# Seven block products in place of eight in the first feed-forward product, residual and hidden layer in DRAM, index scores between projection steps

## What is computed

```python
score = einsum('bqhs,bqh->bqs', relu(einsum('bqhd,bsd->bqhs', q_idx, k_idx)), w_idx)   # 4 index heads of 64
_, sel = top_k(where(causal, score, -inf), 256)
...
h = h + merged @ w_out[i]
n2 = _rmsnorm(h, g_mlp[i])
h = h + square(relu(n2 @ w_ff1[i])) @ w_ff2[i]        # w_ff1 1024 x 4096, w_ff2 4096 x 1024
n3 = _rmsnorm(h, g_ple[i])
h = h + sigmoid(n3 @ w_ple_gate[i]) * (p[i] @ w_ple[i])
```

## Times and profile before

| | us |
|---|---|
| median of three runs | 1805.27 (1805.12 to 1806.44) |
| the profiled execution, its own time | 1806.59 |
| its span, first to last instruction | 1804.8 |

### The profile page before, as it was taken

How to read it: one execution, slowest core, us unless ns; L and a number is a source line. 1 busy time by engine, 2 the same in 40 slices (tenths; PEclk the granted TensorE clock), 3 DMA queues, 4 the chain that set the end, 5 groups by cost and what they waited for, 6 DMA issues and landing times.

```text
span 1804.8 us, 21895 instructions
## 1 busy us (share of the span) xinstructions
PE 1724.0 (96%) x8728; PEld 1362.2 (75%) x8728; DVE 808.2 (45%) x1321; ACT 559.3 (31%) x818; POOL 354.8 (20%) x166
## 2 busy tenths in 40 slices
PE   5899989999899999999998999999999999999997
PEld 4568778787556666678887888888888888888886
DVE  7499999901255576654323412121212222215524
ACT  5422322222355566621222302031211112114223
POOL 2212342122200000212211222222222222222220
PEclk8999999999899999999999999999999999999999
DMA  4202122242100020014320111111111111111112
GB/s 149 79 24 59 35 71 93 82 128 74 47 1 1 1 71 1 2 54 153 120 93 31 46 53 47 46 46 46 46 56 49 46 46 46 46 47 52 42 58 93
DMA packets 90324, 103.08 MB, mean 57 GB/s; under 512 B 15920, under 2 KB 82480, under 8 KB 90256
## 3 DMA queue, kind: packets, MB, share of 16 engines
q1 hardware_dynamic: 87504, 92.70, 16.5%
q10 hardware_dynamic: 2592, 9.44, 1.4%
q0 software_dynamic: 160, 0.02, 0.1%
HBM read 86.54 MB, written 13.76 MB: 56 GB/s over the span
## 4 chain that ended last, share of the span: by engine, by line
PE 90%; DVE 4%; ACT 3%; issue 1%; POOL 1%; DMA 0%; ACTq 0%; DVEq 0%; POOLq 0%
PE ps L1479 73%; PE ps L1697 3%; PE ps L1711 3%; PE ps L1662 2%; PE ps L1681 2%; PE ps L1668 2%; PE ps L1576 2%; PE ps L1776 1%; DVE sc L1174 1%; DVE prob_a L1303 1%; PE ps L1638 1%; DVE prob_b L1303 1%; DVE tmp L1450 0%; PE ps L1507 0%; POOL w_lo L660 0%
## 5 line engine op out<-in xcount | busy, mean ns | idle before, releaser
L660 POOL TENSOR_TENSOR w_lo<-w_raw,w_hi 128x1024 fp32r<-128x1024 f32 x131 | 315.7, 2411 | 1115.8 <-ACT w_hi L744 1115.8
L744 ACT ACTIVATE w_hi<-w_raw 128x1024 fp32r<-128x1024 f32 x131 | 138.7, 1061 | 929.5 <-PE ps L1479 883.1
L1479 PE MATMUL ps<-n_hi,w_hi 128*128 128x512 f32 x1120 | 351.3, 395 | 23.3 <-DVE n_lo L1372 6.6
L1479 PE MATMUL ps<-n_lo,w_hi 128*128 128x512 f32 x1120 | 349.0, 393 | 0.0
L1479 PE MATMUL ps<-n_hi,w_lo 128*128 128x512 f32 x1120 | 348.5, 393 | 0.0
L1479 PEld LDWEIGHTS ps<-n_hi,w_hi 128*128 128x128 f32 x1120 | 212.8, 191 | 71.3 <-issue 11.1
L1479 PEld LDWEIGHTS ps<-n_lo,w_hi 128*128 128x128 f32 x1120 | 213.1, 190 | 45.0
L1479 PEld LDWEIGHTS ps<-n_hi,w_lo 128*128 128x128 f32 x1120 | 212.8, 190 | 44.8
L1401 DVE TENSOR_TENSOR h<-h,ps 128x2048 f32<-128x2048 f32 x32 | 73.2, 2287 | 221.6 <-PE ps L1479 221.6
L1187 DVE TENSOR_SCALAR_CACHE_REDUCE tested<-sc,bar_i 128x384 bf16<-128x384 f32 (+2 forms) x192 | 169.0, 942 | 1.7 <-POOL sc L675 0.6
L1479 PE MATMUL ps<-hid_lo,w_hi 128*128 128x512 f32 x512 | 157.6, 389 | 0.0
(11 more groups left out here) (261 smaller groups left out, 2025.8 us busy)
## 6 DMA issues: line engine op xcount, KB each, us to landing
w_raw<-in_w_ff_dram SPq DMA_DIRECT2D x64, 512.0 KB, 3.5
w_raw<-in_w_in_dram SPq DMA_DIRECT2D x28, 512.0 KB, 3.7
gates_scratch<-stage ACTq DMA_DIRECT2D x16, 512.0 KB, 2.6
sig_ab<-gates_scratch SPq DMA_DIRECT2D x8, 1024.0 KB, 5.9
x_tok<-in_x_dram SPq DMA_DIRECT2D x8, 512.0 KB, 10.1
w_raw<-in_w_out_dram SPq DMA_DIRECT2D x8, 512.0 KB, 4.9
xs<-in_x_dram SPq DMA_DIRECT2D x4, 1024.0 KB, 5.0
w_raw<-in_w_ple_gate_dram SPq DMA_DIRECT2D x8, 512.0 KB, 3.4
```

Source lines behind the costliest of these rows:

```text
L660: pool.tensor_tensor(w_lo[s][:, :, :], w_raw[s][:, :, :], w_hi[s][:, :, :].bitcast(F32), ALU.subtract).then_inc(lo_ready, 1)
L744: act.activation(w_hi[s][:, :, :], w_raw[s][:, :, :], ACT.Copy).then_inc(hi_ready, 1)
L1479: last = pe.matmul(bank(4 * half + 2 * j + t)[0:w, :], wm, xm[:, t * HALF:(t + 1) * HALF], start=(k == 0 and a), stop=(k == total - 1 and ...
```

## The change

1. **First feed-forward product.** The input channels are divided into even and odd row tiles, a unit of 256 hidden columns into two column tiles, the tokens into two halves. A unit is so a 2 x 2 block product, and it is done with seven products of blocks in place of eight. A product (P1 to P7) is 4 row tiles x 3 matmuls over 512 tokens. Block sums of the weights (`s_raw`, four for each unit) and of the activations (T1 to T4, once) are made on VectorE and, for unit 0, on GpSimd. P1, P6, P7 and P4 accumulate one after another in bank 0 of the unit's half of PSUM, and ScalarE copies what stands there after P1, P6 and P7 (`copy_chain`). P2 lies in bank 1, P5 and P3 in bank 2. VectorE adds the copies to the other banks (`add_c11`, `add_c22`, `add_c12`) and applies relu and the norm's factor; C21 is taken from bank 0 after P4 (`take_c21`). Products of neighbouring units are interleaved in the order of `PRODUCTS`.
2. **Order of the feed-forward.** All 16 units of the first product run first; each hidden tile is squared and stored to DRAM (`hid_d`). Then the second product runs in eight passes of four groups, loading four hidden tiles for each pass, two buffers of four, and splitting them into high and low (`hid_high`, `hid_low`).
3. **Residual.** Each quarter of h is written to DRAM (`h_d`) after the output projection and read back before the second product. The load of p, its transposes and their parts move behind the first pass of the second product. The buffers of high, low and raw parts lie at other places of SBUF.
4. **Index scores.** One unit is now at most 512 keys of one pair of heads in its own two banks; after each of the units 1 to 16 comes a sixteenth (`qa_step`, 6 matmuls) of the first of the four projections. A high part is made ahead of the second sine, one at unit 12 and one after the scores; a low part ahead of the last mask.

The core of the diff (in this order: scratch tensors and product order, SyncE, GpSimd, ScalarE, VectorE, TensorE's index scores, TensorE's first product):

```diff
+    h_d = nc.dram_tensor("h_scratch", (D // P, P, S), F32, kind="Internal").ap()
+    hid_d = nc.dram_tensor("hid_scratch", (FF // P, P, S), F32, kind="Internal").ap()
...
+        UNITS_1 = FF // WCOL
+        B11, B21, B22, T1, T2, T3, T4 = range(7)
+        SECOND = {"P1": B11, "P2": B21, "P3": B22, "P4": T4, "P5": T1, "P6": T2, "P7": T3}
+        PRODUCTS = [(0, "P1"), (0, "P2"), (1, "P1"), (1, "P2"), (0, "P6"), (0, "P5"), (0, "P7"), (1, "P6"), (0, "P4"),
+                    (0, "P3"), (1, "P5"), (1, "P7"), (2, "P1"), (2, "P2"), (1, "P4"), (1, "P3")]
+        for u in range(2, UNITS_1):
+            PRODUCTS += [(u, "P6"), (u, "P5"), (u, "P7")]
+            PRODUCTS += [(u + 1, "P1"), (u + 1, "P2")] if u + 1 < UNITS_1 else []
+            PRODUCTS += [(u, "P4"), (u, "P3")]
...
+            for u in range(2, UNITS_1 + 1):
+                sp.wait_ge(a_lo_done, POS[u - 2, "P4"] + 1)
+                wait_sum(sp, u - 2, 4)
+                if u < UNITS_1:
+                    load_unit(u)
+                else:
+                    load_ff2(0)
+                    load_ff2(1)
+                if u >= 3:
+                    store_unit(u - 3)
+            sp.wait_ge(a_used, POS[UNITS_1 - 1, "P2"] + 1)
...
+            store_unit(UNITS_1 - 1)
+            sp.wait_ge(a_used, LAST)
+            sp.wait_ge(c12_done, UNITS_1)
+            for b in range(2):
+                sp.wait_ge(hid_stored[b], 32 * (UNITS_1 // 2))
...
+            load_h(0)
+            for k in range(CHUNK):
+                load_hid(1, k)
+            for q in range(1, 2 * OUT_N):
+                load_h(q)
             sp.dma_start(p_tok[:, :, :], p2.rearrange("(t q) d -> q t d", q=P)).then_inc(p_loaded, 16)
...
+            for n in range(2, 4 * FFN):
+                if n % 4 == 2 and 1 <= n // 4 < FFN - 1:
+                    sp.wait_ge(slab_used, FF2_SLAB + 4 * (n // 4))
+                    for k in range(CHUNK):
+                        load_hid(n // 4 + 1, k)
+                load_ff2(n)
...
+            def first_lo(o):
+                pool.wait_ge(a_hi_done, o + 1)
+                pool.tensor_tensor(a_lo[o % 10][:, :, :], first_of(o), a_hi[o % 10][:, :, :].bitcast(F32),
+                                   ALU.subtract).then_inc(a_lo_done, 1)
...
+            pool.tensor_tensor(s_raw[0][:, :, :], block_of(0, "A21"), block_of(0, "A22"), ALU.add).then_inc(s_first, 1)
...
+                    act.activation(n_pair[:, c, :], tile_ps(half, c), ACT.Copy,
+                                   scale=g_mlp_c[:, 2 * q + c:2 * q + c + 1]).then_inc(n_done, 1)
...
+                    act.activation(gated[:, :, :], hp[:, :, :], ACT.Square).then_inc(h_sq, 1)
+                    act.dma_start(h_d[2 * q:2 * q + 2].rearrange("a q n -> q a n"), hp[:, :, :]).then_inc(h_spilled, 16)
...
+            HI_AT = {0: (6,), 4: (7, 8), 5: (9, 10), 6: (11,), 7: (12, 13)}
+            for o, (u, name) in enumerate(PRODUCTS):
+                if name in ("P1", "P6", "P7"):
...
+                    copy_chain(u, name)
+                for ahead_o in HI_AT.get(o, ()) if o < 8 else (o + 6,):
...
+                        first_hi(ahead_o)
+                if o == 7:
+                    act.wait_ge(sq_summed, 1)
...
+                        act.activation(rms[:, t * HALF:(t + 1) * HALF], bank(4 * t + 3), ACT.Sqrt, bias=eps_c,
+                                       scale=1.0 / D).then_inc(root_done, 1)
+                if name == "P3" and u < UNITS_1 - 1:
+                    hid_square(u, 1)
+                if o >= 1 and PRODUCTS[o - 1][1] == "P3":
+                    hid_square(PRODUCTS[o - 1][0], 0)
...
+            add_c11(0)
+            sums_of_blocks(1)
+            add_c11(1)
+            add_c22(0)
+            inverse(2)
+            relu(0, 0, first, c11_done)
+            relu(1, 0, first, c11_done)
+            relu(0, 1, second, c22_done)
+            last_sum(1)
+            take_c21(0)
+            add_c12(0)
+            relu(0, 0, second, c12_done)
+            sums_of_blocks(2)
...
+            for u, (i, pair, c, w) in enumerate(IDX_UNITS):
...
+                if u >= 2:
+                    pe.wait_ge(rel_done, 2 * (u - 1))
...
+                if 1 <= u <= 2 * DT:
+                    qa_step(u - 1)
+            pe.wait_ge(rel_done, 2 * len(IDX_UNITS))
+            for _ in range(3):
                 project()
...
+            PLACE = {"P1": 0, "P6": 0, "P7": 0, "P4": 0, "P2": 1, "P5": 2, "P3": 2}
...
+                    if name in ("P1", "P2", "P5") and u >= 2:
+                        pe.wait_ge({"P1": c21_done, "P2": c11_done, "P5": c12_done}[name], u - 1)
+                    if name in ("P6", "P7", "P4"):
+                        pe.wait_ge(u_copied, COPY_AT[u, {"P6": "P1", "P7": "P6", "P4": "P7"}[name]] + 1)
+                    if name == "P3":
+                        pe.wait_ge(c22_done, u + 1)
...
+                    for w, x, a, z in ((a_hi, b_hi, True, False), (a_hi, b_lo, False, False), (a_lo, b_hi, False, True)):
+                        last = pe.matmul(unit_bank(u, PLACE[name]), w[o % 10][:, j, :], x[j][:, b, :],
...
+            for o in range(4):
+                first_product(o, range(0, KT - 1))
+            for o in range(4):
+                first_product(o, range(KT - 1, KT))
+            for o in range(4, LAST):
+                first_product(o, range(0, KT))
+                if o == 6:
+                    square_sums((3, 7), SQ3)
```

More of the change, by code:

```diff
@@ L1029, in out_weights @@
-            def out_weights():
+            for i in range(FFN):
                 for q in range(4):
                     hi_parts(1)
-                    at_.group(1)
-            root(1)
-            hidden(0, 0)
-            out_weights()
-            with act.Fori(0, FFN - 2) as i:
-                at_.loop(i, 8, 6)
-                ahead.loop(i, 8)
-                hidden(i, 1)
-                out_weights()
-                at_.end(FFN - 2)
-                ahead.end(FFN - 2)
-            hidden(0, FFN - 1)
@@ L1057, in _ @@
+                if i == 0:
+                    half = group()
+                    act.activation(pt_hi[:, :, :].rearrange("q a n -> q (a n)"), bank(4 * half, 4), ACT.Copy).then_inc(
+                        pt_hi_done, 1)
+            root()
             for q in range(2 * OUT_N):
@@ L1515, in _ @@
             project(((0, P),))
-            for half in range(2):
-                freed(pe, half, at_.groups // 2)
+            half = group()
+            freed(pe, 1 - half, (at_.groups) // 2)
             for t in range(TT):
@@ new lines, in _, with first_project, sums @@
+            for o in range(4):
+                first_product(o, range(0, KT - 1))
+            for o in range(4):
+                first_product(o, range(KT - 1, KT))
[3 more added lines that the diff above has]
+                    square_sums((3, 7), SQ3)
+            def first_project():
+                half = group()
+                g = at_.groups
+                def sums():
+                    freed(pe, g % 2, free_count(g - 2))
+                    square_sums((4 * (g % 2), 4 * (g % 2) + 1), SQ3 + DT)
+                product(half, FULL, (KT, KT), residual, first_wait=lambda k: pe.wait_ge(norm_lo, k + 1),
+                        after=lambda k: sums() if k == DT - 3 else None)
+                pe.wait_ge(root_done, 3)
@@ new lines, in ff2_product @@
+            def ff2_product(i, q):
+                half = group()
+                if i == 0 and q < 2:
+                    u = UNITS_1 - 2 + q
+                    pe.wait_ge(c11_done, u + 1)
+                    pe.wait_ge(c12_done, u + 1)
+                    pe.wait_ge(c21_done, u + 1)
+                product(half, FULL, (KT,), lambda k: (hid_hi[i % 2][k][:, :], hid_lo[i % 2][k][:, :]),
+                        first_wait=(lambda k: pe.wait_ge(hid_lo_done, CHUNK * i + k + 1)) if q == 0 else None)
@@ L1818, in feed_forward @@
+            assert at_.slabs == FF2_SLAB and (at_.groups - OUT_GROUP) % 2 == 0
+            for i in range(FFN):
                 for q in range(4):
+                    ff2_product(i, q)
+                if i == 0:
                     half = group()
-                    product(half, FULL, (KT,), lambda k: (hid_hi[:, k, :], hid_lo[:, k, :]),
-                            first_wait=hid_there if q == 0 else None)
-            feed_forward(0, 0)
-            with pe.Fori(0, FFN - 1) as i:
-                at_.loop(i, 8, 6, 6)
-                feed_forward(i, 1)
-                at_.end(FFN - 1)
+                    pe.wait_ge(p_loaded, 16)
+                    for f in range(2):
+                        for t in range(TT):
+                            last = pe.transpose(bank(4 * half + 2 * f, 2)[:, t * P:(t + 1) * P],
+                                                p_tok[:, t, f * P:(f + 1) * P], ident[:, :])
+                    last.then_inc(turn_done, 1)
```

586 lines of the change are left out of this document (408 added, 178 removed).

## The result

| | us | ratio to the kernel before, 95% interval |
|---|---|---|
| before, beside it (4 runs) | 1805.86 (1805.12 to 1806.90) | |
| changed kernel (4 runs) | 1783.42 (1781.77 to 1784.99) | 0.9875 [0.9858, 0.9892] |
| forecast | 1773.0 (1755 to 1789) | 0.982 |

The change gains 22.4 us; 32.2 were forecast. The time lies in the range of 1755 to 1789, but above the 1766 to 1780 that the forecast called its own. Of the rivals, (d) with 1782 is nearest: scores that gain nothing and a longer root stop.

A forecast was written before the change was run, and what follows sets the result against it. TensorE, 96% busy, was taken as the bound: fewer matmuls less new stops take the feed-forward stage from 708.6 to 680.9 us. 1806.59 - 27.7 - 4.5 = 1774.4, 1.3 less against the median: 1773, range 1755 to 1789.

The forecast's parts named there:

- (d): Rival: the index scores gain nothing and the root stop in the first feed-forward product doubles; 1782 us, chance 8%.
- (b): Rival: chain copies come late in the first product's steady units, 1 us in each of 14 units; 1787 us, 14%.
- Fewer matmuls: First feed-forward product: 84 matmuls per unit in place of 96, 192 fewer over 16 units, -43.5 us.
- their pace: First product's matmuls stay at 0.2267 us each; 12 in a row to one bank cost nothing extra, bounds 0 and 8 us.
- the steady units: First product: a unit lasts 19.0 us; the other engines' work, chain copies and transfers fit beside TensorE.
- (c): Rival: 12 matmuls in a row to one bank run slower; at 50 ns more each, 1840 us, chance 4%.
- Start of the first product: After the output projection, VectorE and GpSimd exclude each other and P6 comes late: 3.2 us (0.2 to 5).
- Root stop: Before P1 of unit 2, TensorE waits for root, reciprocal and relu: 4.1 us (3 to 7), plus 2.2 of slow speed.
- Last unit: Last unit of the first product: nothing lies between P7 and P4 to cover ScalarE's copy, 1.3 us.
- Queue stop: Before the second product's third group, a weight slab queues behind 7.5 MB: 11.3 us (6 to 17), plus 2.2 slow speed.
- (a): Rival: the load queue at the second product drains unseen, 13.5 us better; 1759.5 us, chance 15%.
- Index scores: First query projection laid between the score matmuls, so that TensorE binds: -4.5 us (-2 to -7).

The follow-up runs named there:

- late steps: Changed kernel with the first projection's 16 steps moved to the last score units: 1780.79 us laid singly, 1775.98 us laid in pairs.
- the root first: Changed kernel with ScalarE taking the root ahead of the copy of P6 of unit 1 and two high parts: 1775.61 us.
- the engines apart: Changed kernel with GpSimd's block sums of unit 0 held until VectorE has made T1 to T4: 1782.24 us.
- the old scores: Changed kernel with the score and projection order, and its high and low parts, put back as in the kernel before: 1782.90 us.

## Why the forecast held, and where it was off

The forecast of 1773.0 was 10.4 us too low; the time is inside the wide range, whose upper end of 1789 had been set by rival (b), and (b) did not happen. The path and both stops were as put, their sizes short; the gain of the index scores did not come.

- **Fewer matmuls, their pace, the steady units**: right. 192 fewer, 1344 at 0.2267, no stop in units 2 to 14. Rivals (b) and (c) are out: nothing waits in the steady units, and 12 in a row to one bank cost nothing.
- **Start of the first product** (term 3.2, up to P6 only): the mutual exclusion is there, 1.8 in place of 0.69 in three operations. Before P6 TensorE stood 1.02 + 0.16 + 0.62. Not foreseen was 1.08 before P7 of unit 0: ScalarE's copy of P6 stood behind its copy of P1 of unit 1, which waited for VectorE's first addition, and that stood behind the additions of the squares (to 983.1). Together 2.9 idle, near the 3.2, but from two causes: that the size came out is in part luck. The two waits:

```profile
983.81 0.60 ACT L1241 ACTIVATE u_one<-ps 128x512 f32<-128x512 f32 x1 [5.20 <-DVE c_out L1683]
...
985.00 0.47 PE L2172 MATMUL ps<-b_hi,a_hi 128*128 128x512 f32 x1 [1.08 <-issue]
```

- **Root stop** (4.1 and 2.2 for the clock): 5.75 and 2.9. The term that was too small is that of the "two high parts" ahead of the root, counted as 1.2 us of ScalarE's work. One of them waited 2.34 us for a load. P1 of unit 2 so began 44.2 us into the stage (1009.12 - 964.9), where the sum had 38.7 + 3.2 = 41.9.
- **Last unit** (1.3): 0.8.
- **Queue stop** (11.3 and 2.2): 12.14 and 3.1, and 0.7 more for VectorE's addition to h behind it. The mechanism and the place are as put, the first slab of the third group behind 7.5 MB; so rival (a) is out. The rate of 0.385 MB per us taken from the earlier trace rows was near: 339 to 419 GB/s here.
- **Index scores** (-4.5): here the forecast fell. Its sum had 43.5 us (16.3 + 21.8 + 3.5 + 1.9) from the first score to the next projection, with the slow start of that projection. The interleaved order took 48.0 (74.78 to 122.82), and the slow start is 1.9 (288 matmuls in 67.22, with late steps in 65.3): 50.0, so 6.5 over. The sum took a score step at its own pace and a projection step at its own, 2.22 us for a unit of 512 keys and its step; they take 2.64 in turn (109.46 to 112.10). The term that was missing is that of the changes: 16 x 0.42 = 6.7 us. The tail without projection had 2.5 us of idleness in place of 3.5; the last 0.8 was not traced. Against the kernel before, which needs 48.3 to the same point by the prediction's count, this is a loss of 1.7, and that it vanishes from the time is due to the faster projections later on, for which the prediction has no term. The half of rival (d) that says that the scores gain nothing came true; its other half, a root stop of twice 4.1, did not (5.75).

In the stage, P1 of unit 2 began 2.3 later than in the sum and its slow start cost 0.7 more; the queue stop and its slow start took 1.7 more, the addition to h 0.7, the last unit 0.5 less. That makes 4.9 of the 5.7 missing; the rest was not traced.

## What to carry to other kernels

When two kinds of matmul are laid between each other to fill idle time, count the changes between them, not only the work, and put the filler where the idle time is: at the end, when the partner engine drains. When the next engine waits for an instruction, count for each instruction ahead of it in its queue also what that one waits for, not only its work. Before a turn through DRAM, issue first what the next product needs and what does not depend on the turn: two slabs moved up in a queue of 7.5 MB were worth 14 us, more than half of what the whole change gained.

## What the runs showed of the hardware

- Going from the 128-row projection matmuls to the 64-row float32 score matmuls and back costs TensorE about 0.42 us with no wait in the records (2.64 for what takes 2.22 apart). Eight fewer such turns brought 2.8 and 3.0 us, 0.34 to 0.38 each. Whether the row size, the type or the weights are the cause was not separated.
- A stop of 1.6 us cost 0.3 afterwards (96 matmuls in 22.04 us in place of 21.8), longer ones more: after 5.8 us the next matmuls lost 2.9, after 12.1 us 96 of them took 24.94. The length alone does not settle it: after the same stop of 12.1 to 12.2 us these 96 took 24.94 in the changed kernel, 24.37 with the root first, 23.43 with the engines apart and 23.39 with the old scores. So this stop cost its own length and 1.6 to 3.2 us more. The granted clock in the windows of the changed kernel, in the long stop and after it:

```profile
1307.00:1319.00 12.00, 0.03 (x1) 0.00 (x0) 1.43 (x1) 3.47 (x4) 2.33 (x2) 0.70 0.71 241
1319.00:1344.00 25.00, 24.83 (x97) 20.27 (x98) 9.06 (x5) 2.44 (x3) 5.75 (x3) 0.87 0.13 43
```

1.00 is 2.4 GHz and 0.5 is 1.2 GHz, so 0.87 is a mean of the two over the stretch behind the stop.
